# Fast two-by-two products in the second feed-forward product of a decoder layer: seven block products for eight on eight of sixteen hidden-feature pairs

## The reference, cut to what matters

```python
def _sq_relu_mlp(h, w_ff1, w_ff2):
    return jnp.square(jax.nn.relu(h @ w_ff1)) @ w_ff2      # h (256, 1024), w_ff1 (1024, 4096), w_ff2 (4096, 1024)

ff = _sq_relu_mlp(x, w_ff1[l], w_ff2[l])
x = _layer_norm(DEEPNORM_ALPHA * x + ff, ln3_g[l], ln3_b[l])
```

## Time and profile before

| | |
|---|---|
| median of three runs (lowest, highest) | 406.16 us (405.75, 406.31) |
| the profiled execution: span of the trace, first to last instruction | 404.4 us |
| the profiled execution's time outside its span, taken as median less span | 1.8 us |
| TensorE busy | 397.4 us, 98% of the span |
| VectorE busy | 286.5 us, 71% |
| ScalarE busy | 208.2 us, 51% |
| GpSimd busy | 64.7 us, 16% |
| mean granted TensorE clock | 0.998 of full speed |
| DMA | 75.68 MB, mean 187 GB/s |

### The profile page before, as it was taken

The page is one execution under the profiler, slowest core; times in us unless marked ns, Lnnn a source line. Parts: engine busy times, 40 slices in busy tenths (PEclk is TensorE's granted clock), DMA queues, the critical chain, the costliest instruction groups (busy, mean ns, idle before and its releaser), DMA issues.

```text
span 404.4 us, 5680 instructions
## 1 busy us (share of the span) xinstructions
PE 397.4 (98%) x2148; PEld 341.3 (84%) x2148; DVE 286.5 (71%) x376; ACT 208.2 (51%) x295; POOL 64.7 (16%) x61
## 2 busy tenths in 40 slices
PE   9999999999999999999999999999999999999993
PEld 6888888888988888899888888888888888888882
DVE  5599584999987896878658858474656466574826
ACT  6666569566464627565743366353534434354500
POOL 2059300047951004000006000000000000000000
PEclk9999999999999999999999999999999999999999
DMA  8998727635635380827166173746465654644002
GB/s 287 376 352 281 254 106 264 255 105 174 243 109 205 108 309 0 311 105 245 68 209 201 46 273 117 256 155 212 199 207 207 207 207 150 237 141 198 0 0 104
DMA packets 31195, 75.68 MB, mean 187 GB/s; under 512 B 1510, under 2 KB 2886, under 8 KB 31174
## 3 DMA queue, kind: packets, MB, share of 16 engines
q1 hardware_dynamic: 30784, 75.24, 53.5%
q10 hardware_dynamic: 390, 0.17, 0.2%
HBM read 74.35 MB, written 1.05 MB: 186 GB/s over the span
## 4 chain that ended last, share of the span: by engine, by line
PE 98%; DVE 1%; DVEq 0%; issue 0%
PE bank L1374 18%; PE bank L1376 18%; PE bank L1375 18%; PE bank L1774 13%; PE bank L1448 12%; PE bank L1781 7%; PE bank L1452 6%; PE bank L1600 2%; PE bank L1380 1%; PE bank L1440 1%; PE bank L1554 1%; PE bank L1587 0%; PE bank L1653 0%; PE bank L1705 0%; PE bank L1546 0%; PE bank L1545 0%
## 5 line engine op out<-in xcount | busy, mean ns | idle before, releaser
L907 DVE TENSOR_TENSOR w_lo<-raw,w_hi 128x2048 fp32r<-128x2048 f32 x36 | 84.5, 2352 | 12.9 <-ACT w_hi L556 12.8
L556 ACT CAST w_hi<-raw 128x2048 fp32r<-128x2048 f32 x38 | 72.1, 1913 | 15.4 <-PE bank L1376 14.3
L1309 DVE TENSOR_TENSOR w_lo<-raw,w_hi 128x2048 fp32r<-128x2048 f32 x24 | 54.4, 2289 | 30.4 <-ACT w_hi L844 30.4
L1374 PE MATMUL bank<-w_hi,actB 128*128 128x512 f32 x192 | 75.6, 394 | 0.0
L1375 PE MATMUL bank<-w_lo,actB 128*128 128x512 f32 x192 | 74.9, 390 | 0.0
L1376 PE MATMUL bank<-w_hi,actB 128*128 128x512 f32 x192 | 74.8, 390 | 0.0
L844 ACT CAST w_hi<-raw 128x2048 fp32r<-128x2048 f32 x24 | 45.4, 1917 | 34.4 <-PE bank L1376 34.4
L1774 PE MATMUL bank<-actA,w_hi 128*128 128x512 f32 x224 | 52.2, 390 | 0.0
L1774 PEld LDWEIGHTS bank<-actA,w_hi 128*128 128x128 f32 x224 | 42.0, 188 | 8.7
L1376 PEld LDWEIGHTS bank<-w_hi,actB 128*128 128x128 f32 x192 | 36.1, 188 | 7.6
L1374 PEld LDWEIGHTS bank<-w_hi,actB 128*128 128x128 f32 x192 | 36.1, 188 | 7.2
(11 more groups left out here) (198 smaller groups left out, 591.3 us busy)
## 6 DMA issues: line engine op xcount, KB each, us to landing
raw<-in_w_ff SPq DMA_DIRECT2D x32, 1024.0 KB, 5.4
raw<-in_w_in SPq DMA_DIRECT2D x10, 1024.0 KB, 6.4
raw<-in_w_xkv SPq DMA_DIRECT2D x8, 1024.0 KB, 5.0
raw<-in_w_mix_o SPq DMA_DIRECT2D x4, 1024.0 KB, 4.8
raw<-in_w_xq SPq DMA_DIRECT2D x4, 1024.0 KB, 4.9
raw<-in_w_xo SPq DMA_DIRECT2D x4, 1024.0 KB, 5.0
raw<-in_lead SPq DMA_DIRECT2D x6, 384.0 KB, 5.1
probs<-in_ln_g SPq DMA_DIRECT2D x3, 512.0 KB, 6.3
```

Of the source, the lines that this page charges most:

```text
L556: act.copy(dst, half_view(u)).then_inc(hi_done, 1)
L907: dve.tensor_tensor(dst, half_view(u), hi_part.bitcast(f32), ALU.subtract).then_inc(lo_done, 1)
L1309: dve.tensor_tensor(w_lo[:, c % 2, half, :], raw[:, u % RAW, :], w_hi[:, c % 2, half, :].bitcast(f32), ALU.subtract).then_inc(lo_done, 1)
L1374: pe.matmul(dst, stat[0], mov[0], start=start, stop=False, skip_group_check=on)
```

## The change

The hidden features are now taken as 16 pairs (`PAIRS`): a pair is two k-tiles of 128 features, 256 rows of `w_ff2`. The activations of a pair form a two-by-two block matrix over (half of the tokens, k-tile), with blocks A11, A12, A21, A22 of 128 by 128, and the weights one over (k-tile, half of the columns), with blocks B11 to B22 of 128 by 512.

- Eight pairs ("S" in `KINDS`) use seven block products on sums of blocks (the form with S1 to S4 and T1, T2, T4, where T3 takes the place of B12 in the raw slot). Seven pairs ("C") use the eight plain products, placed so that they add to the same seven accumulators, with two differences D1, D2 of activation blocks. The last pair ("L") is plain and goes into the four output corners themselves.
- The products P1 to P7 accumulate in banks 0, 3, 2, 1, 4, 5 and 6. The first feed-forward product's blocks share bank 7 (the second block uses bank 6), so a block waits until ScalarE has emptied the one ahead (`empty`).
- VectorE makes the weight sums in float32 (`weight_sums`, four 128 by 512 additions for an S pair), ScalarE casts them (`wsum_high`, 128 by 1536), VectorE subtracts (`wsum_low`). The activation sums are made, cast and subtracted likewise (`hidden_sums`, `asum_high`, `asum_low`). Relu and square move to ScalarE (`square`), the addition of the two halves of a first-product block is one VectorE instruction on SBUF (`add_halves`, 128 by 512).
- TensorE's order is, for each pair q: a block of pair q+2's hidden features (8 matmuls of 512 columns, 8 of 256), half of pair q's products, the other block, the rest. The loops are written out straight on all engines.
- At the end ScalarE copies P1 out, VectorE combines the seven banks into four corners, TensorE adds the last pair to each corner as it is ready, and the layer norm runs for t = 1 first and t = 0 second.
- The host lays `w_ff1` and `w_ff2` out by unit, so that each partition's part of a unit is one contiguous run. Each unit is still 1 MB, and their number does not change.

The diff, cut to its core ("..." marks what is left out):

```diff
+KINDS = "SCSCSCSCSCSCSCSL"
...
+S_PRODUCTS = {"P1": ("A11", "B11"), "P2": ("A12", "B21"), "P3": ("S4", "B22"), "P4": ("A22", "T4"),
+              "P5": ("S1", "T1"), "P6": ("S2", "T2"), "P7": ("S3", "T3")}
+C_PRODUCTS = [("P2", "A11", "B11"), ("P2", "A12", "B21"), ("P4", "A21", "B11"), ("P4", "A22", "B21"),
+              ("P5", "A21", "B12"), ("P5", "A22", "B22"), ("P3", "D1", "B12"), ("P3", "D2", "B22")]
+P_BANK = {"P1": 0, "P2": 3, "P3": 2, "P4": 1, "P5": 4, "P6": 5, "P7": 6}
+FIRST_ORDER = ["P1", "P2", "P4", "P5", "P7", "P6", "P3"]
+ORDER = ["P1", "P2", "P7", "P3", "P5", "P6", "P4"]
+LAST_ORDER = ["P1", "P2", "P3", "P6", "P5", "P7", "P4"]
...
+FF_UNITS = [("down", 0), ("up", 2), ("up", 3), ("down", 1)]
+for _q in range(1, PAIRS - 2):
+    FF_UNITS += [("up", _q + 3), ("down", _q + 1)]
...
+                    was, pair = FF_UNITS[n - RAW]
+                    if was == "up":
+                        sp.wait_ge(up_lo, pair - 1)
+                    else:
+                        sp.wait_ge(down_raw_lo, pair + 1)
+                        if KINDS[pair] == "S":
+                            sp.wait_ge(t4_made, s_rank(pair) + 1)
+                if kind == "down":
+                    src = w_ff2[at_pair]
+                else:
+                    src = w_ff1[at_pair] if at_pair < PAIRS else w_ff2[PAIRS - 1]
+                sp.dma_start(half_view(u), src).then_inc(raw_in[u % RAW], 16)
...
+            def down_high(q):
+
+                u = ff_unit("down", q)
+                act.wait_ge(raw_in[u % RAW], raw_count(u))
+                if KINDS[q] == "S":
+                    act.wait_ge(t3_made, s_rank(q) + 1)
+                if q == 0:
+                    wait_full(act, "cpv3")
+                elif q == 1:
+                    wait_full(act, "hid1")
+                else:
+                    act.wait_ge(pair_used, q - 1)
+                act.copy(down_hi[q % 2][:, 0:2048], half_view(u)).then_inc(down_raw_hi, 1)
...
+            def empty(p, m):
+
+                n = 2 * (p - 2) + m
+                act.wait_ge(up_full, n + 1)
+                if n >= 2:
+                    act.wait_ge(relu_done, p - 2)
+                act.copy(emptied[:, m], bank[6 if n == 1 else 7][:, :]).then_inc(up_free, 1)
+
+            def square(p):
+                act.wait_ge(halves_added, p - 1)
+                act.wait_ge(a_lo, p - 1)
+                act.wait_ge(asum_lo, asum_count(p - 2))
+                v = hidden[p % 2][:, 0:512]
+                act.activation(v.rearrange("p (m s) -> p m s", m=2), emptied[:, :, 0:S], ACT.Relu).then_inc(relu_done, 1)
+                act.wait_ge(relu_done, p - 1)
+                act.activation(v, v, ACT.Square).then_inc(hidden_done, 1)
...
+            up_high(2)
...
+            down_high(0)
             first_relu(0)
+            act.wait_ge(ln_done, 8)
+            seed_product("P4", 0, 1, ALPHA)
+            seed_product("P3", 1, 0, ALPHA)
+            wsum_high(0)
             first_relu(1)
+            wait_out(act, "hid1")
+            seed_product("P2", 1, 1, ALPHA)
+            first_hidden(0)
+            first_hidden(1)
+            hidden_high(0)
+            empty(2, 0)
+            asum_high(0)
+            up_high(3)
+            empty(2, 1)
+            hidden_high(1)
+            down_high(1)
+            asum_high(1)
+            wsum_high(1)
+            for q in range(1, PAIRS - 2):
+                up_high(q + 3)
+                square(q + 1)
+                hidden_high(q + 1)
+                empty(q + 2, 0)
+                down_high(q + 1)
+                asum_high(q + 1)
+                wsum_high(q + 1)
+                empty(q + 2, 1)
+            square(PAIRS - 1)
+            hidden_high(PAIRS - 1)
+            act.wait_ge(product_done, 1)
+            act.copy(first_product, bank[P_BANK["P1"]][:, :]).then_inc(p1_copied, 1)
...
+                t1, t2, t4 = [sums_w[:, n * 512:(n + 1) * 512] for n in range(3)]
+                dve.wait_ge(raw_in[u % RAW], raw_count(u))
+                if r == 0:
+                    wait_full(dve, "cpv3")
+                else:
+                    dve.wait_ge(wsum_lo, r)
+                dve.tensor_tensor(t1, b12, b11, ALU.add).then_inc(t1_made, 1)
+                dve.wait_ge(t1_made, r + 1)
+                dve.tensor_tensor(b12, b12, b22, ALU.add).then_inc(t3_made, 1)
+                dve.tensor_tensor(t2, t1, b22, ALU.add).then_inc(t2_made, 1)
+                dve.wait_ge(t2_made, r + 1)
+                dve.tensor_tensor(t4, t2, b21, ALU.add).then_inc(t4_made, 1)
...
+            def add_halves(p):
+                dve.wait_ge(up_free, 2 * (p - 2) + 2)
+                dve.tensor_tensor(emptied[:, :, 0:S], emptied[:, :, 0:S], emptied[:, :, S:2 * S], ALU.add)\
+                    .then_inc(halves_added, 1)
...
+                link(dve.tensor_tensor(v[:, 512:768].rearrange("p (m s) -> p m s", m=2),
+                                       a21.unsqueeze(1).to_broadcast([P, 2, P]),
+                                       v[:, 128:384].rearrange("p (m s) -> p m s", m=2), ALU.subtract))
+                link(dve.tensor_tensor(s2, a11, s1, ALU.subtract))
+                dve.tensor_tensor(s4, a12, s2, ALU.subtract).then_inc(asum_made, 1)
...
+            up_low(2)
+            weight_sums(0)
+            down_low(0)
             first_square(0)
+            wsum_low(0)
             first_square(1)
+            hidden_sums(0)
+            hidden_low(0)
+            asum_low(0)
+            up_low(3)
+            hidden_sums(1)
+            hidden_low(1)
+            weight_sums(1)
+            down_low(1)
+            asum_low(1)
+            wsum_low(1)
+            add_halves(2)
+            for q in range(1, PAIRS - 2):
+                weight_sums(q + 1)
+                up_low(q + 3)
+                hidden_sums(q + 1)
+                hidden_low(q + 1)
+                down_low(q + 1)
+                asum_low(q + 1)
+                wsum_low(q + 1)
+                add_halves(q + 2)
+            hidden_low(PAIRS - 1)
...
+            b = product("P2")
+            dve.wait_ge(p1_copied, 1)
+            dve.tensor_tensor(b, b, first_product, ALU.add).then_inc(corner_done, 1)
+            link(dve.tensor_tensor(sixth_less_first, product("P6"), first_product, ALU.subtract))
+            link(dve.tensor_tensor(with_fifth, product("P5"), sixth_less_first, ALU.add))
+            b = product("P3")
+            dve.tensor_tensor(b, b, with_fifth, ALU.add).then_inc(corner_done, 1)
+            link(dve.tensor_tensor(with_seventh, product("P7"), sixth_less_first, ALU.add))
+            link(dve.scalar_tensor_tensor(left_rest, X[:, 0, 0:512], ALPHA, with_seventh, ALU.mult, ALU.add))
+            dve.tensor_tensor(bank[P_BANK["P7"]][:, :], product("P5"), left_rest, ALU.add).then_inc(corner_done, 1)
+            b = product("P4")
+            dve.tensor_tensor(b, b, with_seventh, ALU.subtract).then_inc(corner_done, 1)
...
+            last_norm(1, ["P3", "P2"], 0)
+            last_norm(0, ["P7", "P4"], 1)
...
+                n = 2 * (p - 2) + m
+                b = bank[6 if n == 1 else 7]
+                if n == 0:
+                    wait_out(pe, "yt11")
+                elif n == 1:
+                    wait_out(pe, "yt10")
+                else:
+                    pe.wait_ge(up_free, 1 if n == 2 else n)
...
+            up_block(2, 0, between=lambda: transpose_hidden(0))
+            transpose_hidden(1)
+            up_block(2, 1)
+            multiply(0, FIRST_ORDER)
+            for q in range(1, PAIRS - 2):
+                up_block(q + 2, 0)
+                if KINDS[q] == "S":
+                    multiply(q, ORDER[:4])
+                else:
+                    multiply_plain(q, 0)
+                up_block(q + 2, 1)
+                if KINDS[q] == "S":
+                    multiply(q, ORDER[4:])
+                else:
+                    multiply_plain(q, 1)
+            multiply(PAIRS - 2, LAST_ORDER, last=True)
+            pe.wait_ge(a_lo, PAIRS)
+            pe.wait_ge(up_lo, PAIRS - 1)
+            final = blocks[(PAIRS - 1) % 3]
+            for n, (name, t, c) in enumerate([("P2", 1, 1), ("P3", 1, 0), ("P7", 0, 0), ("P4", 0, 1)]):
+                pe.wait_ge(corner_done, n + 1)
+                for m in range(2):
+                    block_at = (2 * m + t) * P
+                    i = three(bank[P_BANK[name]][:, :], [final[:, at0 + block_at:at0 + block_at + P] for at0 in (0, 896)],
+                              [v[:, 1, 0, m * 1024 + c * 512:m * 1024 + (c + 1) * 512] for v in (w_hi, w_lo)],
+                              False, m == 1, on=True)
+                i.then_inc(corner_full, 1)
```

More of the change, by code:

```diff
@@ L68 @@
 N_FRONT = len(CHUNKS)
[L69 to L70 removed]
+C_FF1_0 = N_FRONT
 MEM_CHUNK = 6
@@ L144 @@
              10: "mo11", 11: "xv11", 12: "xq11", 13: "xq3", 15: "xo11", C_FF1_0: "hid1"}
-ROWS_END = {9: 1, 14: 2, C_FF2_0: 3}
-FF_BASE = [sum(b == bank for b, _ in FILL.values()) for bank in range(8)]
+ROWS_END = {9: 1, 14: 2}
```

(34 more changed lines are left out.)

443 lines of the change are left out of this document (242 added, 201 removed).

## The result

The changed kernel takes 406.97 us in the median of 7 runs (406.75 to 407.50), the kernel before, run beside it, 405.93 (405.51 to 406.35). The ratio is 1.0027, with a 95% interval of 1.0017 to 1.0037: slower by 0.27%, 1.0 us. The forecast was 406.6 us with a range of 404.6 to 409.3. Its likeliest class was "within 0.2%" (chance 0.43, slower 0.38); the median lies just outside, on the slower side, and the interval still has 0.2% in it.

The account below looks back on a forecast made before the run. TensorE was taken as the bound, busy 397.4 of 404.4 us. 404.4 - 5.5 + 0.5 + 2.8 + 2.2 + 0.4 = 404.8, with 1.8 around it 406.6 us; range 404.6 to 409.3.

Parts of the forecast that it names:

- Removed: In `ff2` on TensorE, 384 matmuls become 360; 24 at 0.2273 us make 5.5 us less.
- Steady state at zero: Middle of the stage: VectorE's and ScalarE's added work costs zero, as `empty` is ready over 2 us before TensorE wants it.
- The rule that the prediction set against this step: VectorE drains after each operation for about its duration less 266 ns; by that the kernel would be over 80 us slower.
- The start: Stage start: TensorE's transposes wait 1.3 and 0.9 us for the squares, then bank 7 twice; 2.8 us more, bounds 2.0 to 3.8.
- The end: VectorE's combinations and two norms end 6.0 us behind TensorE instead of 3.8: 2.2 us more, bounds 1.5 and 3.4.
- Double waits: VectorE steps behind two waits start 0.10 us after; some six on the start and end chains: 0.4 us, bounds 0 and 1.5.
- Alternation: Blocks of 8 replace blocks of 32: 21 more returns to 512 columns at 0.026 us, 0.5 us more, bounds 0 and 0.6.
- a pace over 0.23: Sign on TensorE that its many satisfied waits, costed at nothing, do cost time.
- the ends overlap better: Faster rival at both ends: late starts vanish, hand-overs are free, alternation costs nothing; 404.2 us, chance 0.22.
- 0.1 us for each dependent step: Slower rival on the VectorE and ScalarE chains at start and end: hand-overs cost 0.10 us; 408.8 us, chance 0.20.
- VectorE becomes the bound in S pairs: Rival: VectorE's lump is over 2 us longer, TensorE waits for bank 7 in steady state; 411 to 416 us, chance 0.09.
- The clock: Rival: TensorE's clock falls, each 10 us at 1.2 GHz doing 5 us of work; 411 us or more, chance 0.02.

Follow-up runs that it names:

- experiment 1: Changed kernel with only two pairs by seven products (the first and pair 14), the six between made plain: 411.11 us, ratio 1.0125 to the kernel before.
- Experiment 10: Changed kernel with all pairs but the last by seven products: 423.92 us, ratio 1.0446 to the kernel before.
- Experiment 2: Changed kernel with relus ahead of the down unit's casts and squares ahead of low parts at the stage's start: 404.99 us, ratio 0.9978 to the kernel before.
- experiment 4: Kernel before, its first product alternating 8 long and 8 short matmuls instead of 32 and 32: 406.26 us, ratio 1.0011.
- experiment 5: Changed kernel in which TensorE waits for each semaphore value only once: 407.34 us, ratio 1.0033 to the kernel before, pace 229.8 ns.
- experiment 9: Changed kernel with the three SBUF places of the activation blocks turned by one: 407.56 us in one run.

## Why the prediction was right, and where it wasn't

- **Removed:** 24 matmuls, 5.5 us. The count is right, and experiment 1 shows the gain in the middle.
- **Steady state at zero:** right. TensorE has no pause between 258 us and its last matmul, and it is busy for 20 of 20 us with VectorE at 16.3. The rule that the prediction set against this step would have made the kernel over 80 us slower, and it is 1.0 us slower. In the chain at the end most of VectorE's dependent steps of 0.69 us follow each other 0.02 us apart. The prediction gave the rule without its exception: the same section of the Trainium skill, "VectorE: DVE Perf Modes", "The DRAIN you can't avoid", says that an operation which isn't held starts earlier. Experiment 10 shows the cover's edge by taking it away: the wait for bank 7 appears, 1 us in each iteration, 13 us in all.
- **The start, 2.8 us:** right in mechanism and place, measured 3.1 over before (1.64 and 0.93 for the two squares against 1.3 and 0.9; 0.5 at 256.5 against 0.1 and 0.5). Experiment 2 takes 2.0 of them back.
- **The end, 2.2 us:** right. Combinations begin 2.4 us after the start of the last S pair's products (forecast 2.35), the two norms take 4.3 each. The forecast's 6.0 us counts TensorE's last matmul as one distance of 0.227 us, its 3.8 for before counts it to the end of its row. By the first count VectorE ends 6.0 us behind now and 4.0 before, by the second 5.9 and 3.8: 2.1 us more by either.
- **Double waits, 0.4 us:** too high. The hand-overs of the chain at the end are 0.02 us, and one is 0.10 (388.57). What they cost is in the measured start and end already.
- **Alternation, 0.5 us:** the term as such is right (experiment 4). What failed is that it stood for all that changes in TensorE's pace, which costs 1.5 us, outside the term's bounds of 0 to 0.6. The forecast named satisfied waits as what could add to it and "a pace over 0.23" as the sign, and 0.227 as the sign of being right. The waits cost nothing (experiment 5), and the pace is 0.2298, under that threshold, in place of the 0.228 that alternation gives. A second cause was missing: the blocks and weights were put in new places in SBUF. The five slow pairs have some 105 matmuls at 5 ns, 0.5 us. Behind each half of such a pair the next block's long matmuls start with 226, 236, 228, 232 and 231 ns before they are back at 227, nine times 20 ns, 0.2 us. The last 0.3 or so is in pairs 2, 5, 8 and 11, which come back later than others, and at the two ends of the stage. That the place of the operands decides is shown for the slow pairs by experiment 9; for the rest it is only what is left, since waits, banks, straight code and VectorE's load fell.

The term of the pace was 1.0 us too low and the start 0.3 too low, the end 0.1 and the double waits 0.4 too high, and the profiled execution came to the stage 0.6 us earlier. That the sum came out at 404.8 against a span of 405.1 owes something to these cancelling: there luck had a part. The median is 0.4 us over the forecast. The class was missed by 0.2 us: the difference between the kernels is 1.0 us where the bound is 0.8, and the forecast had it at 0.4.

Of the rivals, "the ends overlap better" is wrong: the pauses at 256.5 are there. "0.1 us for each dependent step" is wrong, by the hand-overs. "VectorE becomes the bound in S pairs" didn't come, since its lump fitted; experiment 10 is that case. The clock didn't fall here: it is 1.00 from 3.8 us until 399.8, 3.1 us after TensorE's last one, and the run's mean of 0.993 comes from the 0.50 behind that. The Trainium skill, "TensorE: Matmul & The Clock Gate", section "A second HAM failure mode: psum-queue depth-cycling", says that cycling through banks with small idles makes the clock swing. Seven banks are cycled here with pauses of up to 1.64 us, and the rows show no swing. What a longer pause did is in experiment 10: the clock fell to 0.50 behind one of 3.3 us.

Left open: which property of the two places makes the pace (distance, a division of SBUF, the order of reading). No kernel with other addresses for the weights was run. That their slot counts rests on odd pairs in `actB` running at 229 where even ones run at 234, with pairs of one kind in experiments 1 and 10 as well. And the last pair of experiment 9, slow though its block had left `actB`, shows that the two named places aren't the whole rule: whether its own places make it slow, or the slow pace of pair 14, which it follows with no short matmuls between, goes on, is open.

## What to carry to other kernels

A saving on the bound engine is worth what the two ends leave of it: find what the other engines must have done before the bound engine's first and last instructions of the stage, and order their queues by that. Here two such reorderings and a shared norm turned +0.3% into -0.5%, and a little more of the change then paid too, while all of it, without these edits, cost 4%. And when an engine's pace changes by one or two per cent, read single instructions by buffer slot before blaming waits or banks.

## What the runs showed of the hardware that was not expected

The place of a matmul's operands in SBUF sets its pace. With the same shapes, order of banks and clock (1.00), 512-column matmuls that load their own weights stand 234 ns apart in pairs whose activation block is in `actB` and whose moving operand is in the first weight slot, and 229 with the block or the weights elsewhere, in pairs 0 to 14; with the blocks turned, the slow pairs turn with them. The Trainium skill's "TensorE: Matmul & The Clock Gate", section "Step-by-step: what each phase is for", says that loading the next tile's weights takes no read bandwidth from the running matmul. By that alone one wouldn't expect the places to matter. The measurement decides that they do; it doesn't show whether reading is what they share.

Behind matmuls of 256 columns, it takes five of 512 (233, 236, 228, 232, 231 ns) until they are back at 227 in most groups, in straight and in looped code alike. In the block of long matmuls that follows half of a slow pair it takes about five again, with no short ones between (226, 236, 228, 232, 231).

A pause of TensorE of 3.3 us was followed by 3.4 us at a granted clock of 0.50 (experiment 10); pauses of up to 1.7 us were not.
